# Hybrid decoder layer on one core: the value product with values as weights, rows scaled ahead of the turning

## The reference

```python
logits = jnp.einsum('bthd,btkhd->bhtk', qh, ks).astype(f32) * (HEAD_DIM_B ** -0.5)
logits = logits + bias.transpose(0, 3, 1, 2)
logits = jnp.where(valid[:, None], logits, -jnp.inf)
p = jax.nn.softmax(logits, axis=-1)
o = jnp.einsum('bhtk,btkhd->bthd', p.astype(vs.dtype), vs)
...
ub = jnp.einsum('blc,cd->bld', ob * jax.nn.silu(zb), w_up_b)
```

## Time and profile before

| | us |
|---|---|
| median of three runs | 509.43 |
| lowest and highest run | 509.41, 514.22 |
| profiled execution, its own time | 512.63 |
| span of its trace | 510.6 |
| mean granted clock of PE | 0.989 of full |

### The profile page before, as it was taken

The page is one execution under the profiler, slowest core; times in us unless marked ns, Lnnn a source line. Parts: engine busy times, 40 slices in busy tenths (PEclk is TensorE's granted clock), DMA queues, the critical chain, the costliest instruction groups (busy, mean ns, idle before and its releaser), DMA issues. The chain is left out here.

```text
span 510.6 us, 6780 instructions
## 1 busy us (share of the span) xinstructions
PE 483.9 (95%) x2582; PEld 400.0 (78%) x2582; DVE 295.0 (58%) x552; ACT 190.2 (37%) x311; POOL 187.4 (37%) x170
## 2 busy tenths in 40 slices
PE   5899999999999999999979899989999999999993
PEld 2678888889778898887867797878778888888883
DVE  6625589999972343334289757697343405264276
ACT  2534454222342213134174427554086333343000
POOL 2844443334564345454012200311005555596000
PEclk9999999999999999999999799999999999999998
DMA  8535212332102211220202202022204222357012
GB/s 309 195 100 176 82 58 83 112 131 88 48 36 83 84 42 43 82 61 23 83 0 83 82 1 85 4 80 82 83 0 161 86 83 82 106 181 291 0 62 103
DMA packets 15439, 45.68 MB, mean 89 GB/s; under 512 B 2056, under 2 KB 3504, under 8 KB 15408
## 3 DMA queue, kind: packets, MB, share of 16 engines
q1 hardware_dynamic: 14016, 44.06, 25.0%
q10 hardware_dynamic: 1392, 1.20, 0.7%
HBM read 43.14 MB, written 2.11 MB: 89 GB/s over the span
## 5 line engine op out<-in xcount | busy, mean ns | idle before, releaser
L1371 POOL TENSOR_TENSOR w_lo<-w_raw,w_hi 128x512 fp32r<-128x512 f32 (+1 forms) x104 | 135.0, 1325 | 137.1 <-ACT w_hi L659 137.0
L389 PE MATMUL bank<-x_hi,w_hi 128*128 128x512 f32 (+1 forms) x360 | 147.3, 409 | 11.2 <-POOL w_lo L1371 6.2
L390 PE MATMUL bank<-x_lo,w_hi 128*128 128x512 f32 (+1 forms) x360 | 142.2, 395 | 0.0
L391 PE MATMUL bank<-x_hi,w_lo 128*128 128x512 f32 (+1 forms) x360 | 142.1, 395 | 0.0
L389 PEld LDWEIGHTS bank<-x_hi,w_hi 128*128 128x128 f32 (+1 forms) x360 | 68.1, 189 | 32.9 <-POOL w_lo L1371 7.0
L391 PEld LDWEIGHTS bank<-x_hi,w_lo 128*128 128x128 f32 (+1 forms) x360 | 68.1, 189 | 15.8 <-issue 0.8
L390 PEld LDWEIGHTS bank<-x_lo,w_hi 128*128 128x128 f32 (+1 forms) x360 | 68.4, 190 | 13.2 <-issue 0.6
L659 ACT ACTIVATE w_hi<-w_raw 128x1024 fp32r<-128x1024 f32 (+1 forms) x66 | 66.7, 1033 | 14.8 <-DMA w_raw<-in_w_units 7.7
L738 ACT ACTIVATE prob<-prob,nmax 128x128 f32<-128x128 f32 (+3 forms) x32 | 17.8, 556 | 85.0 <-DVE nmax L1051 85.0
L389 PE MATMUL bank<-w_hi,x_hi 128*128 128x256 f32 x128 | 37.3, 292 | 0.0
L391 PE MATMUL bank<-w_hi,x_lo 128*128 128x256 f32 x128 | 36.2, 283 | 0.0
(11 more groups left out here) (163 smaller groups left out, 782.9 us busy)
## 6 DMA issues: line engine op xcount, KB each, us to landing
w_raw<-in_w_units SPq DMA_DIRECT2D x68, 512.0 KB, 4.6
x_raw<-in_x_t SPq DMA_DIRECT2D x8, 256.0 KB, 5.3
x_res<-in_x_tok SPq DMA_DIRECT2D x4, 512.0 KB, 6.7
out<-y_sb SPq DMA_DIRECT2D x8, 256.0 KB, 2.0
t_turned<-t_row SPq DMA_DIRECT2D x1, 1024.0 KB, 7.4
ln_gb<-in_ln_g SPq DMA_DIRECT2D x1, 512.0 KB, 6.0
ln_gb<-in_ln_b SPq DMA_DIRECT2D x1, 512.0 KB, 7.0
w_raw<-in_w_kiwi ACTq DMA_DIRECT2D x1, 288.0 KB, 4.1
```

Source lines behind the costliest of these rows:

```text
L389: nc.tensor.matmul(dst, a_hi, b_hi, start=first, stop=False)
L390: nc.tensor.matmul(dst, a_hi, b_lo, start=False, stop=False)
L391: return nc.tensor.matmul(dst, a_lo, b_hi, start=False, stop=last)
L1371: nc.gpsimd.tensor_tensor(split_target(u, x_lo, w_lo)[:, k, :], raw(u)[:, k, :], split_target(u, x_hi, w_hi)[:, k, :].bitcast(F32), ALU.su ...
```

## The change

The value product is turned round. The values become the weights (64 columns) and the turned probabilities move (128 columns). Two heads go to the two column halves of the array, and the result stands in PSUM with channels as rows, as the gate has them. So the turning of groups, `o_tok` and the common order `TURNS` go. The division can't be applied behind the product any longer. It becomes a scaling of the probabilities on DVE ahead of their turning, by pairs: `invert_sums` and `normalise`, at the end of DVE's work on the pair's quarter, behind the top-k rounds. `turn_probs` waits for it. `prob_t` has four buffers instead of two, and `gate_group` comes one quarter earlier and reads the product's bank.

```diff
-Q_GROUP = [Q_ITEM[4 * n + 3] + 4 for n in range(len(GROUPS))]
+Q_GROUP = [Q_ITEM[4 * n + 3] + 3 for n in range(len(GROUPS))]
...
             def turn_probs(i):
                 b, h = ITEMS[i]
-                n = item_turn(i)
-                pe.wait_ge(exp_done, i + 1)
-                if n >= 2:
-                    wait_turn_out(pe, n - 2)
+                pe.wait_ge(norm_done, i + 1)
+                if i >= 2:
+                    wait_turn_out(pe, i - 2)
...
             def attend(i):
...
-                wait_turn_out(pe, item_turn(i))
+                wait_turn_out(pe, i)
+                wait_turn_out(pe, i + 1)
...
                 for c in range(b + 1):
-                    mm = nc.tensor.matmul(out_bank[n % 2][:, h % 4 * 64:h % 4 * 64 + 64], prob_t[:, i % 2, queries(c)],
-                                          v_b[:, c, h * 64:h * 64 + 64], start=(c == 0), stop=(c == b),
-                                          skip_group_check=True)
-                mm.then_inc(pv_done, 1)
-
-            def turn_group(n):
-
-                m = group_turn(n)
-                pe.wait_ge(out_out[n % 2], n // 2 + 1)
-                wait_turn_out(pe, m - 2)
-                for c in range(2):
-                    mm = nc.tensor.transpose(turn_bank[m % 2][:, queries(c)], o_tok[:, n % 2, queries(c)], id_sb[:])
-                mm.then_inc(turn_full, 1)
+                    for e in range(2):
+                        mm = nc.tensor.matmul(out_bank[n % 2][rows(e), queries(h % 4 // 2)],
+                                              v_b[:, c, (h + e) * 64:(h + e) * 64 + 64],
+                                              prob_t[:, (i + e) % 4, queries(c)], start=(c == 0), stop=(c == b),
+                                              skip_group_check=True)
+                        if c == b:
+                            mm.then_inc(pv_done, 1)
...
-                for i in items_at(q - 2):
+                for i in items_at(q - 2)[::2]:
                     attend(i)
...
             def move_probs(i):
...
-                dve.wait_ge(turn_full, m + 1)
-                if i >= 2:
-                    dve.wait_ge(pv_done, i - 1)
+                dve.wait_ge(turn_full, i + 1)
+                if i >= 4:
+                    dve.wait_ge(pv_done, i - 3)
...
-            def divide_group(n):
...
+            def invert_sums(i):
+
+                dve.wait_ge(exp_done, i + 2)
+                if i >= 4:
+                    dve.wait_ge(norm_done, i - 2)
+                pair = slice(i % 4, i % 4 + 2)
+                nc.vector.reciprocal(prob_rcp[:, pair], prob_sum[:, pair]).then_inc(rcp_done, 1)
+
+            def normalise(i):
+
+                dve.wait_ge(rcp_done, i // 2 + 1)
+                n = (ITEMS[i][0] + 1) * P
+                nc.vector.tensor_scalar(prob[:, i % 2, 0:n], prob[:, i % 2, 0:n], prob_rcp[:, i % 4:i % 4 + 1],
+                                        None, ALU.mult).then_inc(norm_done, 1)
+
+            def gate_group(n):
+
+                g, b = GROUPS[n]
                 dve.wait_ge(pv_done, 4 * n + 4)
...
-                for n in groups_at(q):
-                    divide_group(n)
                 for i in items_at(q - 1):
                     move_probs(i)
...
                 for b, r in rounds.get(q, ()):
                     topk_round(b, r)
+                for i in items_at(q)[::2]:
+                    invert_sums(i)
+                for i in items_at(q):
+                    normalise(i)
```

More of the change, by code:

```diff
@@ L84 @@
 LO_DVE = range(Q_PREP[0] // 4 + 1, Q_MERGE // 4 + 2)
-TURNS = sorted([(q + 1, 0, i) for i, q in enumerate(Q_ITEM)] + [(q, 1, n) for n, q in enumerate(Q_GROUP)])
-TURNS = [t[1:] for t in TURNS]
 ROUNDS = TOPK // 8
@@ L220, in hybrid_kernel @@
         w_idx_done, relu_used, pen_done = sem("w_idx_done"), sem("relu_used"), sem("pen_done")
-        logit_pre, exp_done, rcp_done = sem("logit_pre"), sem("exp_done"), sem("rcp_done")
+        logit_pre, exp_done, rcp_done, norm_done = (sem(n) for n in ("logit_pre", "exp_done", "rcp_done", "norm_done"))
         z_sig, gate_a_done = sem("z_sig"), sem("gate_a_done")
@@ L1079, in gate_group @@
                 z = z_b[:, 2 * g:2 * g + 2, queries(b)]
[L1080 to L1081 removed]
+                nc.vector.tensor_tensor(z, out_bank[n % 2][:, 0:2 * P].rearrange("p (c t) -> p c t", c=2), z,
+                                        ALU.mult).then_inc(out_out[n % 2], 1)
             def forget(p, n):
```

45 lines of the change are left out of this document (12 added, 33 removed).

## The result

The changed kernel takes 516.84 us in the median of four runs (515.89 to 517.86), the kernel before 509.42 beside it. The recorded ratio is 1.0094, 95% interval 1.0051 to 1.0138; the quotient of the two medians is 1.0146, and the kernel before by itself spreads from 509.37 to 514.22. The forecast was 508.2, with a range up to 514.5, so the result is outside it, on the slower side.

What follows compares the result with a forecast made beforehand. PE, busy 95% of the span, was taken as the bound. Terms −3.9 − 1.8 − 3.0 − 2.1 + 5.2 + 0.4 + 4.0 = −1.2 us took 509.4 to 508.2 us; range 502.0 to 514.5.

Steps and rivals of the forecast that it cites:

- the gain side: The forecast's savings together: product −3.9, group turns −1.8, idle ahead of them −3.0, chain behind the last head −2.1.
- The shared port: POOL's instructions hold up DVE's scalings at the ports both use: +4.0 us, bounds 0 and 7.
- The bare latency in the pairs 3 to 15: Turning waits for reciprocal and scaling, 0.50 to 0.71 us; mostly covered by slack, +0.4 us.
- sign of being wrong on the stalls: Wrong if turn_probs waits under 3 us or over 12 in all.
- The product: Value product on PE: records at 0.055 us save 8.3, form-change edges cost 4.4; net −3.9 us.
- Rival 1: The two column strips run one after the other, product 17.6 us; kernel slower at 517.0 us; 6%.
- The group turns: The 16 PE transposes of finished groups, 0.11 us each, go: −1.8 us.
- the idle time ahead: PE's idle time ahead of the group turns, 2.4 us plus overlapping tails, goes: −3.0 us.
- The chain behind the last head: Gating a quarter earlier starts the forget gates earlier, so PE's wait for w_lo goes: −2.1 us.
- The top-k stretch: Pairs 0 to 2: scaling behind two top-k rounds on DVE stalls PE 2.7, 1.2 and 1.5 us; +5.2 net.
- The widest pairs: Pairs 6, 7 and 14: slack of 0.5 to 0.6 us doesn't cover the scaling's 0.71; +0.4 us.
- Rival 3: TensorE's clock: a 2.7 us stall may bring a second slow piece, 510 to 512 us, or the 287 piece goes; 14%.

Runs made afterwards that it cites:

- e2: The changed kernel with the two scalings of a pair on ACT, the reciprocal still on DVE behind the top-k rounds; 509.32 us, ratio 0.9964.
- e1: The changed kernel with reciprocal and scalings, still on DVE, ahead of the top-k rounds; 508.92 us, ratio 0.9949 to the kernel before.
- e3: The changed kernel with the scalings on ACT and the reciprocals on DVE ahead of the top-k rounds; 502.66 us, ratio 0.9827.
- e4: The changed kernel without reciprocal and scaling, so its output is not the layer's; 501.95, 501.94 and 498.82 us, ratio 0.9773.
- e6: e3 with the value product written head after head instead of in turns between the column halves; 505.96 us, ratio 0.9891.
- e5: e3 with the gating of each group one quarter later, as before the change; 502.76, 502.83, 507.51 and 507.53 us, ratio 0.9875.
- e7: e3 with one reciprocal for each head instead of one for a pair; 504.27 us, ratio 0.9858.
- e8: e3 with the reciprocal of pair 0 alone put back behind the two top-k rounds; 508.61 us, ratio 0.9941.

## Why the prediction was wrong, point by point

In short: the gain side was right to 1.3 us. Three steps on the other side failed. The shared port was put at 4.0 us and cost 6.4. The bare latency in the pairs 3 to 15 was put at 0.4 and cost 2.0. The clock had no term in the sum and cost 3.3. The waits of pairs 0 to 2 were 1.5 too low as well. The forecast's own sign of being wrong on the stalls, over 12 us of waits ahead of the turning, came.

**The parts.** I compare attention stretches of the table, with slow pieces taken out (3.3 us in the kernel after, 3.0 in e2). Taking DVE's scalings off the port saves **6.4** from the kernel after to e2 (127.1 − 120.7) and again 6.4 from e1 to e3, where 1.9 of it is the wait ahead of the product. Taking the scaling out of the queue behind the top-k rounds saves **3.6** from the kernel after to e1 and 3.5 from e2 to e3. The bare latency is what is left from e3 to e4: 117.1 − 111.9 = **5.3**. The sum is 15.3, and the whole way from the kernel after to e4 is 127.1 − 111.9 = 15.2, so the parts add up and hardly overlap. With e4's −12.1 the changed kernel should be 3.2 us slower than the one before, the slow pieces aside. By the table it is 130.4 − 3.3 − 121.6 = +5.5 in the attention stretch and 249.4 − 251.9 = −2.5 in the rest, so +3.0. Its two slow pieces make it +6.3, and 509.4 + 6.3 = 515.7 is the profiled run (515.89). The median is 0.9 higher, with granted clocks of 0.983 to 0.986 in the other three runs.

**The terms.** The forecast counted by pairs, so e2 is the one to read it against: there POOL can't touch the scalings, and latency and queue are both in place.

- *The product, net −3.9*: right in kind, 1.1 too small. The records start 0.055 apart, as forecast. The blocks take 11.2 us to the next instruction and 1.4 more in the matmuls ahead of them, against 17.6 before: −5.0. The edges are 16 × 0.24 = 3.8, not 4.4, and the kernel before was dearer than I had it. Rival 1 is out, and so is its ground. The Trainium skill, TensorE: Matmul & The Clock Gate, Part 3, "The mechanism", has weights load beside running matmuls only in another row group, and matmuls start strictly in the order of the program. This case disagrees on both: 160 records that use all rows start 0.055 apart where one strip alone has 0.109, and in e6, by the pace of the starts, records of the second strip start ahead of the last three of the first.
- *The group turns, −1.8, and the idle time ahead, −3.0*: right together. The 16 records took 2.3 us from start to start and the idle time 2.4, or 3.1 with the tails; 0.4 of it comes back at edges that those turns had hidden. With the product that makes 9.9 in the attention stretch, where e4 shows 9.7.
- *The chain behind the last head, −2.1*: right in size (the first 35 us of the rest are 2.4 shorter), wrong in its reason. I wrote that the gating comes a quarter earlier and starts the chain earlier. e5 puts it back a quarter and the chain starts as early, since the gating no longer waits for a turn on PE. The right size was luck to that extent.
- *The top-k stretch, +5.2*: 1.5 too low. In e2 the pairs 0 to 2 wait 6.7 us, and in e3, without the queue, still 1.9. The start of pair 0's scaling was 0.25 us off. In the kernel after PE waits 1.35 and 1.98 ahead of pairs 1 and 2, near the 1.2 and 1.5 forecast. Pair 0 waits 3.7 there and not 2.7, and in e2 2.9, so 0.8 of that is POOL's.
- *The widest pairs, +0.4*: this step failed. I held that pairs with 0.5 to 2.2 us between exponentials and turning cover a need of 0.5 to 0.71. In e2 the pairs 3 to 15 wait 2.0 us (2.4 with the change of form), and in e3 2.7: 0.4 to 0.5 ahead of each of the widest pairs 6, 7 and 14, where I had 0.1 to 0.2, 0.7 ahead of pair 3, where I had none, and 0.12 between the two heads of six pairs, of which I hadn't thought. Part of it belongs to these kernels themselves, since ACT's scalings are slower than free ones on DVE (0.39 and 0.71 us for 128 and 512 columns, against 0.28 and 0.48). How much, no run shows. e7 brings the waits down by 2.3 in all, so waiting for the second head's exponential was a good part.
- *The shared port, +4.0*: of the terms of the sum this one was furthest off. It is 6.4, near the upper bound of 7, even beside the slower scalings that replace it. In the pairs 0 to 2, which I had put at 0.8 because POOL is busy half the time, it is 2.5 (9.2 − 6.7), in the others 3.9 instead of 3.2. I gave a split of POOL between the two scalings half a chance. In the six pairs with a mid-pair wait near 1 us it came, and it came in all three (3, 5 and 11) in which I had seen a split stand ready. The mechanism was right, and so was the page SBUF — State Buffer of the Trainium skill, "SBUF: two separate sides", by which a DVE instruction in a two-port mode and any of POOL exclude each other for their whole length. The trace agrees: 16 scalings of 384 and 256 columns average 1.04 us, where free ones take 0.42 and 0.35 (the latter in e1). The top-k instructions and those that read PSUM keep their length beside POOL (MAX8 of 512 columns 0.69 us, the copy of 512 turned columns 0.69, with and without).
- *Rival 3, the clock*: it belonged into the sum, not beside it. I had seen that a wait of 2.7 us might bring a second piece and that the piece at 287 might go. Both came true, with two pieces instead of one: +3.3 where the comparison is with runs of the kernel before that had none. The piece at 287 was worth more than the 2.0 that I had counted on ten matmuls: by the table 3.1. That the pieces of the kernel after come from its long waits fits e1 and e3, which have neither, but e8's wait without a piece shows that such a wait does not always bring one.

So the forecast of −1.2 was −10.8 and +9.6. Measured were −12.1, +15.3 and +3.3 for the clock, +6.5 in all.

## What to carry to other kernels

Before an elementwise step is moved from a slack place to one that TensorE waits for, count whether its engine shares a port with one that has work ready; if it does, price every instruction of the pair at the neighbour's length, or give it to an engine that the neighbour doesn't hold up (here ACT). Put what TensorE waits for ahead of a long block of independent work in the same queue. And a gain of 2 us in waits can be lost to a slow-clock piece of 3 elsewhere, so compare profiles stretch by stretch, not medians alone.

## What was not expected of the hardware

- PE's two column strips keep separate pace: 0.109 us a record each with 128 columns moved, 0.055 together, and with the strips written one after the other the second starts when three records of the first are left (e6). Going into the product's form and out again costs 0.24 us a block, 0.15 of it inside the block and 0.09 in the matmul ahead.
- With work ready on both, DVE's scalings start about one POOL instruction apart (two of 128 columns in 2.38 us, 1.08 from start to start beside splits of 1.26). That the two engines take turns at the port is my reading of it.
- The times of the same kernel fall on steps of 1.6 and 3.1 us, by whether a slow piece comes at the start-up and in the recurrence. A wait of 2.8 us was followed by one at 132.0 (e2) and not at 133.5 (e8). Why isn't settled.

The quickest complete version that was run is e3: the changed product, the scalings on ACT and the reciprocals ahead of the top-k rounds, 502.66 us, 1.7% under the kernel before by the ratio, 1.3% under its runs at full clock, and 2.6% under the changed one by the two ratios (0.9827 / 1.0094). e7's shorter waits would be worth 2 us more if the late piece could be avoided, which was not tried.
